# One transformer step on one core: in the banded attention's weave, VectorE and ScalarE take the dense step ahead of the attention's step

## What is computed

```python
h = rmsnorm(x, attn_norm_g)
proj = h @ w_in                      # da_q da_k da_v | wa_q wa_k wa_v | xa_q | gates
o_da = diff_attention(...)           # 8 heads of two maps
o_wa = window_attention(...)         # 16 heads, band of 128, ALiBi bias, a sink logit per head
o_xa = memory_attention(...)         # 4 heads over 256 memory rows
gate = sigmoid(gates)
merged = gate0 * (o_da @ w_da_o) + gate1 * (o_wa @ w_wa_o) + gate2 * (o_xa @ w_xa_o)
x = x + merged @ w_out
x = x + expert_choice_ffn(rmsnorm(x), ...)   # 16 experts of 1024 x 2048, three matrices each

def one_block(args):                 # of window_attention
    sc = jnp.where(valid, sc - slopes * dist, -inf)
    p = softmax(concatenate([sc, sinks]))[..., :span]
    return einsum('bhgqk,bkhd->bqhgd', p, vb)
```

## Time and profile before

| | us |
|---|---|
| median of 3 runs | 2701.94 (2701.65 to 2703.44) |
| the profiled execution | 2701.89 |
| its span, first to last instruction | 2699.2 |
| mean granted TensorE clock | 0.938 of full speed |
| TensorE busy (matmuls) | 2302.2 (85%) |
| VectorE busy | 1255.6 (47%) |
| ScalarE busy | 932.8 (35%) |
| chain that ended last | PE 63%, DMA 28%, DVE 6%, ACT 2% |

### The profile page before, as it was taken

The page is one execution under the profiler, slowest core; times in us unless marked ns, Lnnn a source line. Parts: engine busy times, 40 slices in busy tenths (PEclk is TensorE's granted clock), DMA queues, the critical chain, the costliest instruction groups (busy, mean ns, idle before and its releaser), DMA issues.

```text
span 2699.2 us, 37912 instructions
## 1 busy us (share of the span) xinstructions
PE 2302.2 (85%) x16606; PEld 1676.6 (62%) x16606; DVE 1255.6 (47%) x1778; ACT 932.8 (35%) x1528; POOL 54.8 (2%) x40
## 2 busy tenths in 40 slices
PE   8999999556566556666699999999999999998998
PEld 8897785112122111212378888888888888887887
DVE  6567663001000000101287865577656556866655
ACT  6556551000000000000255654455443543743443
POOL 0000000000000000000100000000000000003000
PEclk9999999888878887878899999999999999999999
DMA  7543479999999999999934365665554654313652
GB/s 249 172 156 110 140 281 389 430 432 431 431 430 431 430 431 430 432 431 432 347 110 157 105 224 187 203 234 201 190 187 172 203 184 145 120 60 127 203 187 93
DMA packets 236549, 695.45 MB, mean 258 GB/s; under 512 B 10304, under 2 KB 189888, under 8 KB 221408
## 3 DMA queue, kind: packets, MB, share of 16 engines
q1 hardware_dynamic: 234080, 679.15, 65.9%
q0 software_dynamic: 2016, 13.67, 1.4%
q10 hardware_dynamic: 288, 0.22, 0.0%
HBM read 691.96 MB, written 1.05 MB: 257 GB/s over the span
## 4 chain that ended last, share of the span: by engine, by line
PE 63%; DMA 28%; DVE 6%; ACT 2%; issue 1%; SPq 0%; ACTq 0%; DVEq 0%
DMA af<-in_w_exp_up 18%; PE ps L620 16%; PE ps L622 16%; PE ps L621 16%; DMA af<-in_w_exp_down 9%; PE ps L1765 4%; PE ps L1802 2%; DVE ar L593 2%; PE ps L2771 1%; PE ps L2335 1%; ACT af L1124 1%; DVE af L1163 1%; PE ps L936 1%; PE ps L1232 1%; DVE sm L1202 0%
## 5 line engine op out<-in xcount | busy, mean ns | idle before, releaser
L620 PE MATMUL ps<-ar 128*128 128x512 f32 (+2 forms) x2648 | 926.2, 350 | 7.6 <-DVE ar L3486 2.1
L621 PE MATMUL ps<-ar 128*128 128x512 f32 (+2 forms) x2648 | 906.7, 342 | 0.8 <-issue 0.8
L622 PE MATMUL ps<-ar 128*128 128x512 f32 (+2 forms) x2648 | 907.0, 343 | 0.0
L593 DVE TENSOR_TENSOR ar<-af,ar 128x1024 fp32r<-128x1024 f32 x516 | 609.4, 1229 | 216.4 <-ACT ar L582 216.3
L582 ACT ACTIVATE ar<-af 128x1024 fp32r<-128x1024 f32 x516 | 511.8, 1048 | 130.9 <-PE ps L622 114.2
L620 PEld LDWEIGHTS ps<-ar 128*128 128x128 f32 x2648 | 502.1, 190 | 81.3 <-issue 9.6
L622 PEld LDWEIGHTS ps<-ar 128*128 128x128 f32 x2648 | 502.0, 190 | 59.2
L621 PEld LDWEIGHTS ps<-ar 128*128 128x128 f32 x2648 | 502.7, 190 | 56.4 <-issue 1.5
L1765 PE MATMUL ps<-af 128*32 128x512 f32 x2048 | 322.0, 787 | 230.3 <-DMA af<-in_w_exp_up 153.7
L1765 PEld LDWEIGHTS ps<-af 128*32 128x32 f32 x2048 | 74.9, 139 | 468.6 <-issue 189.3
L1939 DVE TENSOR_TENSOR af<-af,ps 128x512 f32<-128x512 f32 x16 | 11.0, 688 | 534.1 <-ACT af L1849 534.1
(11 more groups left out here) (324 smaller groups left out, 1655.3 us busy)
## 6 DMA issues: line engine op xcount, KB each, us to landing
af<-in_w_exp_gate SPq DMA_DIRECT2D x30, 4096.0 KB, 33.5
af<-in_w_exp_up SPq DMA_DIRECT2D x30, 4096.0 KB, 33.4
af<-in_w_exp_down SPq DMA_DIRECT2D x28, 4096.0 KB, 33.6
af<-in_ffn_w_in SPq DMA_DIRECT2D x88, 1024.0 KB, 5.7
af<-in_ffn_w_out SPq DMA_DIRECT2D x44, 1024.0 KB, 5.2
af<-in_w_in SPq DMA_DIRECT2D x34, 1024.0 KB, 5.3
af<-in_sgu_w_in SPq DMA_DIRECT2D x16, 1024.0 KB, 6.9
af<-in_w_exp_down SPq DMA_DIRECT2D x7, 2048.0 KB, 12.0
```

Source lines behind the costliest of these rows:

```text
L593: e.tensor_tensor(self.WL[load.pair][:, c], self.base(i)[:, c], f_(self.WH[load.pair][:, c]), ALU.subtract).then_inc(*self.dve.inc(("lo", ...
L620: e.matmul(o, lh, rh, start=start, stop=False, skip_group_check=True)
L621: e.matmul(o, lh, rl, start=False, stop=False, skip_group_check=True)
L622: return e.matmul(o, ll, rh, start=False, stop=stop, skip_group_check=True)
```

## The change

In the banded attention's weave the two generators change places, on ScalarE and on VectorE. TensorE's weave is as it was.

```diff
@@ a_mix @@
-        weave(self.a_attention(e, "wa", 8, True, 2, self.a_pv_pair("wa", lambda i: F(self.waq)[:, i, :])), dense_b(), 26, 26)
+        weave(dense_b(), self.a_attention(e, "wa", 8, True, 2, self.a_pv_pair("wa", lambda i: F(self.waq)[:, i, :])), 26, 26)
...
@@ v_mix @@
-        weave(self.v_attention(e, "wa", 8, wa_bias, sink=0), dense_b(), 26, 26)
+        weave(dense_b(), self.v_attention(e, "wa", 8, wa_bias, sink=0), 26, 26)
```

## The result

| | before | the change |
|---|---|---|
| median | 2701.94 us | 2717.89 us (2716.35 to 2720.24, 3 runs) |
| the profiled execution | 2701.89 | 2720.24 |
| its span | 2699.2 | 2718.5 |

The ratio is 1.006, with a 95% interval of 1.0045 to 1.0075: the change makes the kernel slower by 16 us, 12 to 20 by the interval. The forecast was 2720, in a range of 2709 to 2729.

What follows compares the result with a forecast made beforehand. The prediction took TensorE to bound the banded weave: 2701.9 us, plus 14.5 of waits (18.8 new less 4.33 old), plus 3.4 for the clock, gives 2719.8, say 2720. The range was 2709 to 2729.

Steps and rivals of the forecast that it cites:

- A2: TensorE's scores(1): would wait 1.2 us for the bias, which stands behind VectorE's dense conversion.
- A3: TensorE's transposes(0): would wait 5.65 us for normed(0), the largest term.
- A4: TensorE's values(0): would wait 1.75 us, since places(0) stands behind ScalarE's second Tanh.
- A9: TensorE's transposes(2): would wait 3.35 us, since VectorE's dense split stands before normed(2).
- A10: TensorE's values(2): would wait 2.1 us, since places(2) stands behind ScalarE's dense split.
- A18: TensorE's transposes(5): would wait 2.25 us, since normed(5) stands behind VectorE's second dense branch.
- A22: TensorE's values(6): would wait 1.75 us behind ScalarE's Tanh, as at A4.
- the four old waits: TensorE's waits in the banded weave that the change can touch: 0.54, 0.37, 2.49 and 0.93 us, 4.33 in all.
- The clock: Dense matmuls behind TensorE's pauses: three slow stretches at 1.7 us each instead of one, +3.4 us net.
- The half-absorbed rival: Behind the stage, in the DMA-bound experts' stretch: half of the delay is absorbed, 2711 us; chance 0.10.
- all hidden: Behind the stage: the experts' loads are issued independently of the mixer and hide all delay, 2702 us; chance 0.05.
- The dense step first gives TensorE its banks early: Rival in the weave: 4.33 us of waits and 1.7 of slow clock are won, 2695.9 us; chance 0.05.

Runs made afterwards that it cites:

- the last kernel: The kernel before, with the dense step put inside the attention's step at two places: 2697.39 us, ratio 0.998.
- the start undone: The change, but VectorE takes the attention's step first for steps 0 to 2: 2709.57 us, ratio 1.003.
- The filled kernel: The change, with 12, 7 and 3 unused constant matmuls on TensorE in three of its pauses: 2710.97 us, ratio 1.0037.
- the first filled kernel: The change, with 24, 14 and 7 unused constant matmuls on TensorE in the same three pauses: 2724.54 us, ratio 1.0083.

## Why the prediction was right, point by point

- **The bound.** That TensorE sets the stage, and that only its waits count, held: the stage is long where TensorE waits or has the lower clock. Without either it takes 91.6 us (92.88 less 1.30 of waits in the last kernel).
- **A2**, 1.2 us: 1.05. **A3**, 5.65: 5.59. **A4**, 1.75: 1.66. **A9**, 3.35: 3.25. **A10**, 2.1: 1.75; the transposes of D9 ran at the lower clock and took 1.9 us instead of my 0.93, so part of the wait lay under them. With the start undone, at the full clock, it is 1.90. **A15**, 0.55: 0.51. **A18**, 2.25: 2.24. **A22**, 1.75: 1.66. A24 came out at 0.17. A6 has no wait in the rows, but its transposes start 0.41 us behind the last dense matmul instead of 0.24. Sum 17.9, against 18.8 in the prediction. The releasers are the ones named, and the four old waits are gone.
- **Waits less the old ones**, +14.5: +13.6.
- **The clock**, +3.4 net: +3.0 to +4.0. The stage is 17.54 us longer, 13.6 by waits, which leaves 4.0. The filled kernel kept the same late operands at the full clock and was 4.6 shorter; less the 1.5 that the kernel before pays too, that is 3.0. (By the filled kernel the late operands alone cost 110.37 - 97.40 + 1.5 = 14.5 us: in the change some of that delay lies under slow matmuls and is no wait.) But I had counted stretches, three of them; the rows show 13.7 us at the lower level, four times the 3.4 of before. Part of them lay under waits, at A9 and A10 above all, so they cost 4.6 / 4 = 1.1 us apiece instead of my 1.7. The count was wrong and the price was too high, and the two nearly cancelled. That this term came out right was luck. How many stretches follow a given pause the experiments leave open (one in the kernel with the start undone and three in the change, at nearly the same waits before A9 and A10).
- **What passes on**, all of it: 16.8 us at the first expert and 17.0 at 2340 us. The chain's step to the DMA, which I had expected to come as much later, starts 15.1 us later and ends 17.0 later. The half-absorbed rival (2711) lies outside the measured runs and has nothing in the trace for it; *all hidden* is out.
- **The dense step first gives TensorE its banks early**: it does, at all four places, and the 4.33 us of old waits are gone. The rival failed where the text said it would be decided, at A3, where 0.2 us of spare time had 6.4 us put in front.
- The sum, 2719.8, is 2 us above the median of 2717.89. The stage is 17.5 us longer where the sum had 17.9. The medians differ by 16, 1.6 less than the stage, and that lies within the 3.9 us over which the three runs spread.

## What to carry to other kernels

When several engines run hand-written orders, compare for each part how long before its use it is done, and look at what a reordering puts in front of it: an instruction that itself waits for the consumer holds back everything behind it, however idle the engine is. Here it mattered more that the orders matched than which of them it was: changed on two of the three engines the same rule cost 16 us, on the third alone 37, on all three 5. And a step can be split where its urgent part ends. Putting the dense step there was worth 5 us at two places, where either whole order left a wait; at a third place the part behind it turned out to be urgent too, and it cost 1.02 us.

## What the runs showed of the hardware

- A matmul of 128x256 on float32 operands with the constant weights of `t_idle` appears as two instructions, 24 of them take 10.4 us (219.25 to 229.61 in the first filled kernel), 0.216 us for each instruction.
- Single pauses of 2.24 and 1.66 us (A18, A22 of the change) were followed by matmuls at full rate, 1.09 and 1.08 us for eight, and the single one of 2.49 us of the kernel before by 3.4 us at the lower level. Pauses of 3.25 and 1.75 us close together went with 10.3 us at the lower level in the change, and 3.25 and 1.90 with 3.4 us in the kernel with the start undone.
- An order that matched on all three engines did not keep the clock up: 0.93 from A0 to A25, with pauses of 4.6, 2.5 and 0.7 us.
- With filler matmuls in the pauses the granted clock stayed at 1.00 through the whole stage, and that was worth 4.6 us with the operands as late as in the change.
